# Two blocks with expert-choice feed-forward on one core: each 2 MB expert weight block sent as two transfers of 1 MB, with a wait of TensorE in the middle of each block

## The reference, cut to what matters

```python
def expert_choice_ffn(h, w_router, w1, w3, w2):
    n_tok, d = h.shape[1], h.shape[2]
    cap = EC_FACTOR * n_tok // N_EXPERTS            # 2 * 256 // 16 = 32
    aff = jax.nn.softmax(jnp.einsum('bnd,de->bne', h, w_router).astype(jnp.float32), axis=-1)
    gate, idx = lax.top_k(jnp.swapaxes(aff, 1, 2), cap)
    xs = jax.vmap(lambda hb, ib: hb[ib])(h, idx)
    a = jnp.einsum('becd,edf->becf', xs, w1)
    b = jnp.einsum('becd,edf->becf', xs, w3)
    y = jnp.einsum('becf,efd->becd', jax.nn.silu(a) * b, w2) * gate[..., None].astype(h.dtype)
    return jax.vmap(combine)(y, idx)                # adds each expert's rows back to its tokens
```

## Time and profile before

| | us |
|---|---|
| median of 3 runs | 2176.4 |
| lowest and highest of them | 2175.36 and 2182.8 |
| the profiled execution | 2174.08 |
| its span in the profile | 2172.3 |
| TensorE (PE) busy in it | 1840.8 |
| VectorE busy, ScalarE busy | 409.2, 337.4 |
| granted TensorE clock, mean over the span | 0.942 |

### The profile page before, as it was taken

One profiled execution on the slowest core, in us unless ns is written; L12 is line 12 of the kernel. 1 busy time (PEld: TensorE's weight loads), 2 busy tenths in 40 slices (PEclk: granted clock), 3 DMA queues, 4 the chain that ended last, 5 costly groups with the idle time before them and its releaser, 6 DMA issues.

```text
span 2172.3 us, 23835 instructions
## 1 busy us (share of the span) xinstructions
PE 1840.8 (85%) x10382; PEld 1111.4 (51%) x10382; DVE 409.2 (19%) x1018; ACT 337.4 (16%) x688; POOL 70.7 (3%) x82
## 2 busy tenths in 40 slices
PE   7999999999998999998998888888999655555655
PEld 4566688778786346555432222225578422222223
DVE  3101311100012036433111011113232200000002
ACT  4101320100101135221110000003232000000001
POOL 0001201000000000000000000000140000000000
PEclk9999999999998999998999999999999888888788
DMA  9323743466543246422999999994322599999996
GB/s 409 122 72 126 296 146 145 189 247 267 225 151 116 78 155 233 156 78 102 428 428 428 427 428 428 428 427 173 144 89 78 240 428 427 428 427 428 427 427 271
DMA packets 42152, 582.41 MB, mean 268 GB/s; under 512 B 4673, under 2 KB 4929, under 8 KB 6081
## 3 DMA queue, kind: packets, MB, share of 16 engines
q1 hardware_dynamic: 42048, 580.90, 65.4%
HBM read 579.83 MB, written 1.05 MB: 267 GB/s over the span
## 4 chain that ended last, share of the span: by engine, by line
PE 60%; DMA 34%; DVE 4%; ACT 1%; issue 1%; POOL 1%; SPq 0%; DVEq 0%; ACTq 0%; POOLq 0%
PE banks L577 41%; DMA ring<-in_experts_dram 33%; PE banks L1089 5%; PE banks L1110 3%; PE banks L523 2%; PE banks L509 2%; PE banks L860 2%; PE banks L910 1%; PE banks L562 1%; PE banks L537 1%; DMA ring<-in_weights_dram 1%; DVE banks L1739 1%; DVE hT L1777 0%; PE banks L1177 0%; POOL arena L2393 0%
## 5 line engine op out<-in xcount | busy, mean ns | idle before, releaser
L1089 PE MATMUL banks<-ring,arena 128*32 128x256 f32 (+1 forms) x3072 | 401.7, 528 | 184.8 <-DMA ring<-in_experts_dram 183.0
L577 PE MATMUL banks<-hT,ring 128*128 128x256 f32 (+2 forms) x1776 | 408.3, 391 | 16.0 <-ACT hT L1361 14.0
L577 PEld LDWEIGHTS banks<-hT,ring 128*128 128x128 f32 (+1 forms) x1776 | 337.4, 191 | 90.7 <-issue 46.1
L1089 PEld LDWEIGHTS banks<-ring,arena 128*32 128x32 f32 (+1 forms) x3072 | 145.9, 136 | 438.9 <-DMA ring<-in_experts_dram 257.2
L1110 PE MATMUL banks<-ring,arena 128*32 128x256 f32 (+1 forms) x1536 | 186.8, 489 | 61.3 <-DMA ring<-in_experts_dram 44.5
L577 PE MATMUL banks<-ring,hT 128*128 128x512 f32 (+1 forms) x448 | 173.3, 547 | 0.0
L577 PE MATMUL banks<-arena,ring 128*128 128x256 f32 (+2 forms) x656 | 170.2, 421 | 2.7 <-POOL arena L2401 1.6
L1110 PEld LDWEIGHTS banks<-ring,arena 128*32 128x32 f32 (+1 forms) x1536 | 70.1, 126 | 161.5 <-issue 78.4
L577 PEld LDWEIGHTS banks<-arena,ring 128*128 128x128 f32 (+1 forms) x656 | 123.0, 188 | 49.5 <-issue 32.8
L577 PEld LDWEIGHTS banks<-ring,hT 128*128 128x128 f32 x448 | 80.1, 190 | 91.4 <-issue 91.2
L577 PE MATMUL banks<-arena 128*128 128x64 f32 (+3 forms) x736 | 115.9, 304 | 11.9 <-POOL arena L2395 5.9
(11 more groups left out here) (271 smaller groups left out, 1154.4 us busy)
## 6 DMA issues: line engine op xcount, KB each, us to landing
ring<-in_experts_dram SPq DMA_DIRECT2D x192, 2048.0 KB, 25.6
ring<-in_weights_dram SPq DMA_DIRECT2D x73, 2048.0 KB, 8.0
ring<-in_weights_dram SPq DMA_DIRECT2D x8, 1408.0 KB, 6.5
ring<-in_weights_dram SPq DMA_DIRECT2D x2, 1152.0 KB, 20.9
cT<-in_ctx_dram SPq DMA_DIRECT2D x2, 1024.0 KB, 7.9
ring<-in_weights_dram SPq DMA_DIRECT2D x2, 1024.0 KB, 12.9
ring<-in_weights_dram SPq DMA_DIRECT2D x1, 1536.0 KB, 23.4
xT<-in_x_dram SPq DMA_DIRECT2D x1, 1024.0 KB, 8.1
```

Of the source, the lines that this page charges most:

```text
L577: ins = mm(dst, a, b, start=(i == 0), stop=(i == len(terms) - 1))
L1089: ins = mm(banks[M * q:M * q + M, which, 0:W], xc[:, 4 * half + k, :], w[:, k, W * q:W * q + W], start=(half == 0 and k == 0), stop=(half ...
```

## The change

Each expert block is cut along its free dimension into two halves of two chunks k each: 128 partitions x 2048 fp32, 1 MB, 8 KB in a partition. In HBM the halves now stand one behind the other, each contiguous. SP starts two transfers per block after the same wait on `experts_pe` as before; the first raises `arrived[slot]`, the second a new semaphore `second_half[slot]`. TensorE waits for `arrived` ahead of chunk 0, as before, and for `second_half` ahead of chunk 2, between two matmuls that add to the same PSUM bank. The arithmetic, its order, the slots and the releases of slots stay.

```diff
@@ expert_blocks
-        parts.append(a.reshape(DEPTH2, E, 2, 4, P, FF).transpose(0, 1, 2, 4, 3, 5).reshape(DEPTH2, E, 2, P, 4 * FF))
-    return np.stack(parts, axis=2).reshape(DEPTH2, E, 6, P, 4 * FF)
+        parts.append(a.reshape(DEPTH2, E, 4, 2, P, FF).transpose(0, 1, 2, 4, 3, 5).reshape(DEPTH2, E, 4, P, 2 * FF))
+    return np.stack(parts, axis=2).reshape(DEPTH2, E, 6, 2, P, 2 * FF)
@@ two_blocks
         arrived = [flag(f"weights_in_slot_{s}") for s in range(SLOTS)]
+        second_half = [flag(f"second_half_in_slot_{s}") for s in range(SLOTS)]
@@ TensorE, experts
-                            yield half, ring[:, slot, :].rearrange("p (k n) -> p k n", n=FF)
+                            yield half, slot, ring[:, slot, :].rearrange("p (k n) -> p k n", n=FF)
...
-                        for half, w in stage_in(which):
+                        for half, slot, w in stage_in(which):
                             for k in range(4):
+                                if k == 2:
+                                    eng.wait_ge(second_half[slot], 16 * n)
                                 for q in range(G):
...
-                    for half, w in stage_in(2):
+                    for half, slot, w in stage_in(2):
                         for k in range(4):
                             kk = 4 * half + k
+                            if k == 2:
+                                eng.wait_ge(second_half[slot], 16 * n)
@@ SP, experts, part
-                    eng.dma_start(ring[:, slot, :], t["experts"][l, e, j]).then_inc(arrived[slot], 16)
+                    src = t["experts"][l, e, j]
+                    eng.dma_start(ring[:, slot, 0:2048], src[0]).then_inc(arrived[slot], 16)
+                    eng.dma_start(ring[:, slot, 2048:4096], src[1]).then_inc(second_half[slot], 16)
```

## The result

| | before | changed |
|---|---|---|
| median, us | 2175.88 (6 runs) | 2191.65 (6 runs) |
| lowest and highest | 2174.37 and 2183.28 | 2189.72 and 2194.57 |
| ratio to before, 95% interval | | 1.0066, 1.0052 to 1.0080 |
| span of the profiled execution | 2172.3 | 2192.4 |
| granted TensorE clock in it, mean | 0.942 | 0.921 |

The change makes the kernel slower, by 15.8 us between the medians and 0.66% by the ratio. The forecast was 2180.9 with a range up to 2189.0, so it missed. What came true is the side "slower by over 0.5%", which I had given a chance of 0.14.

What follows compares the result with a forecast made beforehand. The prediction took queued expert-block transfers at 428 GB/s to bound the kernel. Ends -1.8 and -1.0 us plus smaller pieces +7.3 gave +4.5, so 2176.4 + 4.5 = 2180.9 us, range 2173.5 to 2189.

Steps and rivals of the forecast that it cites:

- What bounds the kernel: Expert parts of both layers: queued DMA transfers at 428 GB/s set the length; only work after the last landings counts.
- the rows of 8 KB: Every expert block moves as 256 pieces of 8 KB, not 128 of 16 KB: 41 ns a block, +7.3 us.
- The signs that I had named: Profile after the change: 27648 more SP packets, DMA share 1.00 or more, 424 to 425 GB/s, six-block round 29.6 us.
- The end of layer 0: Behind the last awaited landing, expert 15's fourth block: half a block less matmul work, 1.8 us gained.
- The end of layer 1: Behind the very last block's landing: half of 1.98 us of matmul goes, 1.0 us gained.
- The added waits: TensorE, 192 more waits riding on matmuls: at most 0.15 us at the tails, put at nothing.
- rival C: End of layer 1: lower TensorE clock doubles the work after the last landing, +8.2 us, 2189.1 us; chance 0.05.
- The added issues: SP, 192 more transfer issues of 0.328 us each: covered by the full queue, nothing.
- B: Expert transfers: smaller pieces cost the full difference seen at the start, +11.8 us, 2188.2 us; chance 0.10.

Runs made afterwards that it cites:

- The first experiment: Kernel before, each expert block still one 2 MB transfer on one semaphore, but its HBM source stands as two halves, so pieces are 8 KB: 2190.04 us against 2175.87.

## Why the prediction was wrong

**What bounds the kernel** was read rightly. In both parts the DMA share stayed at 1.01 in every kernel at 427 or 421 GB/s, the round followed the rate, and a change in TensorE's waiting from 228 to 189 us bought nothing.

**The step that failed is the sum's last term, the rows of 8 KB.** I had 0 and 81 ns a block as ends and took 41. Measured were 73 to 77, so the term is 180 x 0.075 = 13.5 us and not 7.3. The trace of before had it: 421 and 422 GB/s were right to the last digit, and I discounted them because a stretch of 3 us is short. (That 8 KB a partition occur only at the start was wrong besides: two weight blocks of the mixers, of 1024 KB each, have it too, and I left them out.) The lower end had no row behind it at all; "the rate is set by bytes" was an assumption. Between a bound that a row shows and one that nothing shows, the middle is no estimate. The first experiment, with no finer wait and nothing gained at the ends, is 14.2 us above the kernel before between the medians. The signs that I had named say the same: the packets are as counted, but the rate is 421 GB/s and not 424 to 425, and the round 29.82 us and not 29.6.

The Trainium skill's fixed cost (DMA: Bandwidth & Descriptors, "Why small descriptors are slow (HBM only)"), by which I had estimated 38 ns a block, points the right way and is half of what the runs show. It agreed with my middle, which made the middle look better founded than it was. (The 6.8 and 7.3 us that the prediction calls the sum there are this one term; the sum was 4.5.)

**The end of layer 0** was right: 1.7 us against 1.8 forecast. **The end of layer 1** was not: 1.0 us less work, at half the clock, and 1.65 us more in the combines; forecast -1.0, measured +1.6 in the profile. With these the sum is -1.7 + 1.6 + 13.5 = +13.4 us. The ratio gives +14.4 with an interval of 11.3 to 17.4, so the sum now lies within it. The end of layer 1 is known from one profile of the change alone.

**The added waits** cost nothing where they stand, as said. I had not seen that over a whole part they lower the granted clock, 0.81 to 0.74 in layer 1, and that it is back at 0.81 with both waits ahead of the block; I had it only as rival C, at the end. It is off the path inside the part, where a block at 1.2 GHz still fits into its 4.97 us.

**The added issues** on SP cost nothing: with even and odd partitions there are as many of them at 428 GB/s.

**The range** failed for a second reason. B (+11.8) and C were listed as if one excluded the other, and the upper end was put at either alone. Both came, B nearly in full and C in part, and together they are above it.

**Not settled:** 2.5 us in the mixer between the layers, where nothing was changed. Its 32 matmuls of line 1182 (line 1177 before) took 8.78 us there, against 7.09 before. The kernel with the old order in HBM has 2.4 us there as well, and the two with pieces of 8 KB that wait ahead of the block 0.9. The 2 us more in layer 1's part are not settled either. The 2.7 us before the first expert need be no effect of the change: that point moved between 1009.4 and 1017.7 us from profile to profile, and by 2.0 us between two profiles of the kernel before.

## What to carry to other kernels

Where the DMA share is 1.00 and a full queue stands behind it, count a transfer in contiguous runs: here halving them cost some 9 ns per added run. Cutting the transfer without cutting the runs was free with even and odd partitions and halved the rate with lower and upper ones, so look at the GB/s beside the share, which was full in both. Ask of a finer wait what hangs behind the last landing; only that can be gained, once per stream, while finer pieces are paid in every transfer. If a resource is at its limit, look for any stretch of the old trace in which it handles the new size, and believe it over a rule of bytes.

## What the runs showed of the hardware

| piece, KB | pieces per engine and 2 MB | round of six blocks, us | one block, us | rate, GB/s |
|---|---|---|---|---|
| 32 | 4 | 29.13 | 4.855 | 431 |
| 16 | 8 | 29.38 | 4.897 | 427 to 428 |
| 8 | 16 | 29.82 | 4.970 | 421 |
| 4 | 32 | 30.74 | 5.123 | 409 |

4, 8 and 16 more pieces cost 42, 73 and 153 ns, 9 to 11 ns each. At 8 KB they cost the same in one transfer as in two; 32 KB ran only in transfers of 4 MB and 4 KB only in transfers of 512 KB. Carried on to no pieces at all, by an estimate with 9.6 ns each, a block would take 4.855 - 4 x 0.0096 = 4.82 us, 435 GB/s. That is the ceiling that the Trainium skill gives (DMA: Bandwidth & Descriptors, "Where 436 GB/s comes from"), and the measured series points to it.

Transfers into 64 neighbouring partitions ran at 212 GB/s with all engines counted busy, and transfers into every second partition at 428. Why is not shown; that the lower and the upper half each reach only half of SBUF's inputs is a guess that fits both runs. The Trainium skill says of two transfers to disjoint partition halves that they serialize and aren't worth it (DMA: Bandwidth & Descriptors, "Rules for kernel authors"). Lower and upper halves were worse here than one full-rate transfer after the other, with half the rate and a ratio of 1.38; even and odd ones ran at the full rate.
